# Gate projections between the convolution's projections, scan steps spread over both, and the second gate's tile in one place of the weight ring

## What is computed

```python
h = rms_norm(x, norm_mix)
p = h @ w_in       # columns: conv x | conv B | conv C | ssm u | gate_a | gate_b
gates = sigmoid(gl + gate_bias)
ya = (bg * (causal_conv3(cg * xc) + conv_b)) @ w_conv_out
s_t = a_bar * s_(t-1) + b_bar * u_t          # complex, 32 groups x 64 states
y = gelu(Re(C s_t) + d * u_t)
yb = (y @ w_glu_a) * sigmoid(y @ w_glu_b)
x = x + (gates[0] * ya + gates[1] * yb) @ w_o
x = x + hier_moe(rms_norm(x, norm_ffn))
out = rms_norm(x, norm_final)
```

## Time and profile before

| | before |
|---|---|
| median of 3 runs | 775.52 us |
| lowest, highest | 775.19, 777.94 us |
| span of the profiled execution | 773.0 us |
| TensorE (PE) busy | 625.0 us, 81% |
| VectorE (DVE) busy | 206.9 us, 27% |
| GpSimd (POOL) busy | 92.5 us, 12% |
| ScalarE (ACT) busy | 79.9 us, 10% |
| moved | 242.26 MB, mean 313 GB/s |

### The profile page before, as it was taken

How to read it: one execution, slowest core, us unless ns; L and a number is a source line. 1 busy time by engine, 2 the same in 40 slices (tenths; PEclk the granted TensorE clock), 3 DMA queues, 4 the chain that set the end, 5 groups by cost and what they waited for, 6 DMA issues and landing times.

```text
span 773.0 us, 8709 instructions
## 1 busy us (share of the span) xinstructions
PE 625.0 (81%) x3637; PEld 369.0 (48%) x3637; DVE 206.9 (27%) x415; ACT 79.9 (10%) x150; POOL 92.5 (12%) x92
## 2 busy tenths in 40 slices
PE   7996999599999998989875885794695596597483
PEld 6885778487887664544430341251151152043041
DVE  3969999755301116001010010010000000000002
ACT  3100010013211004100020000020000011000001
POOL 5094636211000001100000000000000000000000
PEclk9998999799999999999998897898898799898887
DMA  8984530822296236899999999999999999999991
GB/s 245 382 278 167 208 120 0 326 109 109 89 410 235 109 135 238 341 409 408 408 410 410 410 409 409 410 410 410 409 409 410 410 409 409 410 410 410 409 380 56
DMA packets 76423, 242.26 MB, mean 313 GB/s; under 512 B 9618, under 2 KB 9710, under 8 KB 76398
## 3 DMA queue, kind: packets, MB, share of 16 engines
q1 hardware_dynamic: 75534, 238.77, 79.3%
q10 hardware_dynamic: 864, 3.15, 1.2%
HBM read 240.86 MB, written 1.05 MB: 313 GB/s over the span
## 4 chain that ended last, share of the span: by engine, by line
PE 41%; DMA 37%; DVE 12%; issue 3%; SPq 3%; POOL 2%; ACT 1%; POOLq 0%; DVEq 0%
PE bank L1077 16%; DMA ring<-in_w_up 15%; DMA ring<-in_w_gate 15%; PE bank L1310 7%; PE bank L1331 4%; PE bank L1189 3%; DMA ring<-in_w_down 3%; DMA rot_region<-in_w_down 3%; SPq L422 3%; PE bank L1055 3%; PE bank L1343 1%; DVE x_region L865 1%; PE bank L1283 1%; DVE x_region L862 1%; DVE conv_region L843 1%
## 5 line engine op out<-in xcount | busy, mean ns | idle before, releaser
L1310 PE MATMUL bank<-ring,z_region 128*32 128x512 f32 x832 | 124.7, 738 | 88.1 <-DMA ring<-in_w_up 54.7
L1077 PE MATMUL bank<-x_region,ring 128*128 128x256 f32 x688 | 154.1, 384 | 0.2 <-DMA ring<-in_w_in 0.2
L1077 PEld LDWEIGHTS bank<-x_region,ring 128*128 128x128 f32 x688 | 130.6, 192 | 22.8 <-issue 4.4
L1310 PEld LDWEIGHTS bank<-ring,z_region 128*32 128x32 f32 x832 | 26.6, 126 | 180.0 <-DMA ring<-in_w_up 73.3
L1055 PEld LDWEIGHTS bank<-ident 128*128 128x128 f32 x496 | 60.3, 199 | 29.9 <-issue 25.5
L1055 PE MATMUL bank<-ident 128*128 128x128 f32 x496 | 65.6, 289 | 4.3 <-POOL ident L465 4.3
L1011 DVE TENSOR_TENSOR z_region<-z_region,bank 128x512 f32<-128x512 f32 x8 | 8.2, 1027 | 220.6 <-ACT z_region L672 220.6
L537 POOL TENSOR_TENSOR stat<-stat,halfneg 128x1 f32<-128x1 f32 x2 | 1.1, 560 | 456.4 <-DVE stat L717 456.4
L1331 PE MATMUL bank<-ring,m_region 128*32 128x512 f32 x320 | 49.0, 741 | 6.1 <-ACT m_region L674 5.5
L1015 DVE COPY m_region<-bank 128x512 f32<-128x512 f32 x8 | 5.5, 691 | 137.4 <-PE bank L1331 137.4
L1077 PE MATMUL bank<-z_region,ring 128*128 128x256 f32 x128 | 31.3, 403 | 8.2 <-DVE z_region L845 8.2
(11 more groups left out here) (231 smaller groups left out, 517.9 us busy)
## 6 DMA issues: line engine op xcount, KB each, us to landing
ring<-in_w_up SPq DMA_DIRECT2D x28, 2048.0 KB, 23.6
ring<-in_w_gate SPq DMA_DIRECT2D x24, 2048.0 KB, 23.5
ring<-in_w_down SPq DMA_DIRECT2D x20, 2048.0 KB, 23.6
ring<-in_w_in SPq DMA_DIRECT2D x11, 2048.0 KB, 13.7
x_region<-in_w_down SPq DMA_DIRECT2D x8, 2048.0 KB, 23.7
rot_region<-in_w_gate SPq DMA_DIRECT2D x4, 2048.0 KB, 23.3
s_region<-in_w_up SPq DMA_DIRECT2D x4, 2048.0 KB, 23.5
rot_region<-in_w_down SPq DMA_DIRECT2D x4, 2048.0 KB, 23.5
```

Of the source, the lines that this page charges most:

```text
L1077: ins = MM(dst, w[:, k, n * P:(n + 1) * P], rhs[:, k, :], start=k == 0, stop=k == kn - 1)
L1310: ins = MM(bank[4 + w % 2][q, :], xT[:, k, q], wt[:, e, 512 * kk:512 * kk + 512], start=k == 0, stop=k == KD - 1)
```

## The change

1. The list is now one of named items (`x`, `b`, `c`, `ga`, `gb`, `co`). Gate A of tile n stands between B and C of tile n + 2, and gate B of tile n behind that C (`GATE_LAG = 2`); gates 6 and 7 follow behind tile 7, and the eight output projections (`co`) come last.
2. The 18 steps stand behind items 4 + 9t // 4, that is every 2.25 items, up to item 42 (before: every 2, up to item 38).
3. Gate A's Sigmoid goes straight into `mixed`; VectorE multiplies it with the output projection out of PSUM. ScalarE's copy of the output projection is gone. The gates use the half bank that x has just been copied out of.
4. Gate B's Sigmoid goes to place 7 of the ring (`gate_b`), since `z_sb` is still in use. The mixer's ring has seven places (`MIX_RING`), the units of the columns come as x, B, C, gate A, gate B for tiles 0 to 3 and then 4 to 7, and the expert unit for place 7 waits for `mixed_ready`. The order of the places for expert units is another, with 7 and then the last mixer unit's place at the end of the ring's.

```diff
-    for g in range(N_MAIN):
-        order.append(("main", g))
-        if g >= 4 and g % 2 == 0 and step < ST + S5_LAG:
+    mains = []
+    for j in range(KD):
+        mains += [("x", j), ("b", j)]
+        mains += [("ga", j - GATE_LAG)] if j >= GATE_LAG else []
+        mains += [("c", j)]
+        mains += [("gb", j - GATE_LAG)] if j >= GATE_LAG else []
+    for n in range(KD - GATE_LAG, KD):
+        mains += [("ga", n), ("gb", n)]
+    mains += [("co", n) for n in range(KD)]
...
+        while step < ST + S5_LAG and g == 4 + step * 9 // 4:
             order.append(("s5", step))
...
+        gate_b = ring[:, MIX_RING, 0:KD * T].rearrange("p (k t) -> p k t", k=KD)
...
-        order = [RING, RING + 1] + [(MIX_UNITS + i) % RING for i in range(RING)] + [RING + 2]
+        order = [RING, RING + 1] + [(MIX_UNITS + i) % MIX_RING for i in range(MIX_RING - 1)] + [MIX_RING, (MIX_UNITS - 1) % MIX_RING, RING + 2]
...
-        U_U, U_XBC, U_CO, U_GA, U_GB, U_GLU, U_WO = 0, 1, 7, 9, 11, (13, 15), (14, 16)
+        U_U, U_PARTS, U_CO, U_GLU, U_WO = 0, {"x": 1, "b": 2, "c": 3, "ga": 4, "gb": 5}, 11, (13, 15), (14, 16)
...
+        def gate_bank(what, n):
+
+            if n + GATE_LAG < KD:
+                return 2 * (n % 2)
+            return 0 if what == "ga" else 2
...
-                if u >= RING:
-                    sp.wait_ge(units_used, u - RING + 1)
+                if u >= MIX_RING:
+                    sp.wait_ge(units_used, u - MIX_RING + 1)
...
+                        elif last < 0 and SLOT_OF[v] == MIX_RING:
+                            sp.wait_ge(mixed_ready, KD)
                         elif last < 0 and SLOT_OF[v] < RING:
-
-                            sp.wait_ge(units_used, MIX_UNITS - RING + v - 1)
+                            sp.wait_ge(units_used, last_mix_unit(SLOT_OF[v]) + 1)
...
+                elif what == "ga":
                     act.wait_ge(ga_psum, n + 1)
-                    if n >= 2:
-                        act.wait_ge(ga_used, n - 1)
-                    nc.scalar.activation(gate[:, n % 2, :], bank[n % 4][:, 0:T], ACT.Sigmoid,
+                    nc.scalar.activation(mixed[:, n, :], bank[gate_bank("ga", n)][:, 0:T], ACT.Sigmoid,
                                          bias=cols[:, R_GATEB + n:R_GATEB + n + 1]).then_inc(ga_ready, 1)
...
+                elif what == "co":
+                    dve.wait_ge(ya_psum, n + 1)
                     dve.wait_ge(ga_ready, n + 1)
-                    V.tensor_tensor(mixed[:, n, :], mixed[:, n, :], gate[:, n % 2, :], ALU.mult).then_inc(ga_used, 1)
+                    V.tensor_tensor(mixed[:, n, :], bank[n % 4][:, 0:T], mixed[:, n, :], ALU.mult).then_inc(ya_ready, 1)
...
+                elif what == "ga":
+                    if n + GATE_LAG < KD:
+                        pe.wait_ge(xs_ready, n + GATE_LAG + 1)
...
+                    if n + GATE_LAG < KD:
+                        pe.wait_ge(ga_ready, n + 1)
...
             pe.wait_ge(y_ready, YB)
-            pe.wait_ge(gb_ready, KD)
             for n in range(KD):
+                if n < 2:
+                    pe.wait_ge(ya_ready, 6 + 2 * n)
```

More of the change, by code:

```diff
@@ L29 @@
 RING = 8
+MIX_RING = 7
 MIX_UNITS = 17
@@ L55 @@
 EVEN_BANKS, ODD_BANKS = (0, 1, 4, 5), (2, 3, 6, 7)
[L57 removed]
 N_LOGITS = NEG + NE
 S5_LAG = 2
+GATE_LAG = 2
 def mixer_schedule():
+    mains = []
[7 more added lines that the diff above has]
+    mains += [("co", n) for n in range(KD)]
     order, step = [], 0
[L66 to L68 removed]
+    for g, main in enumerate(mains):
+        order.append(main)
+        while step < ST + S5_LAG and g == 4 + step * 9 // 4:
             order.append(("s5", step))
             step += 1
[L71 to L73 removed]
+    assert step == ST + S5_LAG
     return order
@@ L308, in mix_slot, with last_mix_unit @@
         def mix_slot(u):
-            return ring[:, u % RING, :]
+            return ring[:, u % MIX_RING, :]
         def transfers_to(slot, units):
-            return sum(2 if u in U_GLU else 1 for u in units if u % RING == slot)
+            return sum(2 if u in U_GLU else 1 for u in units if u % MIX_RING == slot)
+        def last_mix_unit(slot):
+            return max(u for u in range(MIX_UNITS) if u % MIX_RING == slot)
         def mix_loaded(eng, u):
-            eng.wait_ge(loaded[u % RING], 16 * transfers_to(u % RING, range(u + 1)))
+            eng.wait_ge(loaded[u % MIX_RING], 16 * transfers_to(u % MIX_RING, range(u + 1)))
         def w8(u):
@@ L1144, in main @@
-                if g in (11, 23):
-                    owed[0] += 3
-                if g >= 24 and g % 4 == 3:
+                    if n % 4 == 3:
+                        owed[0] += 1
+                    return
+                unit = U_PARTS[what] + 5 * (n // 4)
+                s = 2 * (n % 2)
+                if what == "x":
+                    if n == 0:
+                        pe.wait_ge(cols_ready, 3)
+                    if n >= 2:
+                        pe.wait_ge(z_ready, n - 1)
+                    if n >= 2 + GATE_LAG:
+                        pe.wait_ge(gb_ready, n - 1 - GATE_LAG)
+                    dst, done = bank[s][:, 0:T], xbc_psum
+                elif what == "b":
+                    dst, done = bank[s + 1][:, 0:T], xbc_psum
+                elif what == "c":
+                    dst, done = bank[s + 1][:, T:2 * T], xbc_psum
+                elif what == "ga":
+                    if n + GATE_LAG < KD:
+                        pe.wait_ge(xs_ready, n + GATE_LAG + 1)
+                    else:
+                        pe.wait_ge(gb_ready, KD - GATE_LAG - 1)
+                        pe.wait_ge(ga_ready, n)
+                    dst, done = bank[gate_bank(what, n)][:, 0:T], ga_psum
+                else:
+                    if n + GATE_LAG < KD:
+                        pe.wait_ge(ga_ready, n + 1)
+                    else:
+                        pe.wait_ge(gb_ready, n)
+                    dst, done = bank[gate_bank(what, n)][:, 0:T], gb_psum
@@ L1147, in main @@
+                if (what, n) == ("x", 1):
+                    pe.wait_ge(u_ready, YB)
+                mix_loaded(pe, unit)
+                project(dst, w8(unit), n % 4, hT, done)
+                if n % 4 == 3:
                     owed[0] += 1
```

88 lines of the change are left out of this document (27 added, 61 removed).

## The result

| | before | changed |
|---|---|---|
| median | 775.66 us (4 runs) | 758.46 us (4 runs) |
| lowest, highest | 775.19, 777.94 us | 756.54, 758.73 us |
| span of the profiled execution | 773.0 us | 754.8 us |
| TensorE (PE) busy | 625.0 us, 81% | 615.8 us, 82% |
| ScalarE (ACT) busy | 79.9 us, 10% | 80.9 us, 11% |

The ratio is 0.977, with a 95% interval from 0.975 to 0.979: 17.2 us faster. The forecast was 763.4, with a range down to 761.2, so the kernel is 2.7 us faster than the range allowed. The direction and the mechanism are as forecast; one term of the sum is not, and a second piece, the larger, was not in the sum at all.

What follows compares the result with a forecast made beforehand. TensorE's arrival at the experts, which releases the full-rate expert-unit stream, was taken as the bound. 13.76 - 1.3 - 0.3 = 12.1 us off the 773.0 span gives 760.9, plus 2.5 to the median: 763.4 us, range 761.2 to 768.5.

Steps and rivals of the forecast that it cites:

- What bounds the kernel: Gap-free expert-unit stream from the issue at 315.07, which waits for TensorE; moving TensorE's arrival moves the end by as much.
- What is not changed: Same arithmetic, and the 6.58 us wait before 68.92 for step 1 stays, with the slow clock behind it.
- What goes, 13.76: TensorE waits removed from the mixer, counted from 68.92: 8.20 + 3.36 + 1.59 + 0.61 = 13.76 us.
- the four: Wait before 145.88 (8.20), slow clock after it (3.36), wait before 105.53 (1.59), wait for the last gate's Sigmoid (0.61).
- The cover of the 8.20: Work between C 7 and output projection 0, 19.6 us, hiding the last convolution; cover put at over 10 us.
- What comes, 1.3 + 0.3: New TensorE wait for gate A's Sigmoid before gate B 2, taken as 1.3 us, plus 0.3 for seams.
- The walk to gate B 2: Gate B 2 due at 116.6, gate A's Sigmoid done at 117.7: wait about 1.1 us, between 0 and 3.4.
- The 0.3 for seams: Allowance in the mixer of 0.3 us for seams that a walk does not see.
- no new waits, below 761.7: Rival: no new waits at all and small ones elsewhere gone, 13.8 us or more off; chance 0.05.
- The dearer table switches: Part of the rival that Gelus hold the mixer's gates longer: 767 us, limit 768.4; chance 0.14.
- Late expert units: Rival: early expert units, one fewer in the ring, come late; up to 10.3 us more, 773.7; chance 0.05.
- waits that come back through ScalarE: Rival: VectorE, slowed under GpSimd's rotations, delays Gelus that hold the gates; 785.9 us, slower than before; chance 0.03.

Runs made afterwards that it cites:

- the two-later experiment: Changed kernel with scan steps from step 2 on one or two items later, so two projections stand where TensorE waited 7.1 us: 747.72 us, ratio 0.964.
- The experiment with the gates behind: Changed kernel without interleaving: x, B, C of all eight tiles, then all 16 gate projections, then the output projections: 760.48 us, ratio 0.981.
- The runs with the code shifted: Do-nothing TensorE instructions added: before with 4, 16, 2 more 772.12, 772.61, 772.68 us; changed with 16 more 756.95, with two fewer in all 760.72.

## Why the prediction was right and wrong, step by step

**What bounds the kernel: right.** The stream of expert units is full from the first release on, and the release moved with TensorE's arrival: 14.85 us at the GLU, 14.90 at the release, 14.49 at the last landing.

**What is not changed: right.** The gap at 68 stayed (7.14), with products of 2.08 and a slow pair behind it. That the sum may leave it out was right for a comparison; as the two-later experiment shows, it was the largest thing left in the mixer, and its row had stood there from the start.

**What goes, 13.76: right.** From the products at 68 to the GLU the changed kernel takes 13.95 us less (13.9 over all profiles, the slow pair left out). Each of the four is absent in the timeline of after. The cover of the 8.20 had been put at over 10 us. VectorE ended the last convolution tile at 177.6 and output projection 0 began at 194.63: 17 us. The experiment with the gates behind shows that this step is most of the gain.

**What comes, 1.3 + 0.3: the first step that failed.** Measured are 0 and 0. The place was right. In VectorE's timeline step 4 and the convolution behind it:

```profile
91.43 0.69 DVE L864 TENSOR_TENSOR x_region<-bank,rot_region 128x512 f32<-128x512 f32 x1 [7.53 <-PE bank L1177]
...
92.75 0.92 DVE L868 TENSOR_TENSOR x_region<-x_region 128x256 f32<-128x256 f32 x1
93.60 2.15 DVE L869 TENSOR_TENSOR x_region<-x_region 128x256 f32<-128x256 f32 x1
...
95.78 2.73 DVE L871 TENSOR_TENSOR_SCAN x_region<-s5c,x_region 128x256 f32<-128x256 f32 x1
...
100.45 0.42 DVE L847 TENSOR_TENSOR conv_region<-bank,conv_region 128x256 f32<-128x256 f32 x1
```

beside GpSimd's last three rotations of the third group:

```profile
91.46 1.93 POOL L514 TENSOR_TENSOR rot_region<-s_region 128x1024 f32<-128x1024 f32 x1
93.35 2.11 POOL L515 TENSOR_TENSOR x_region<-s_region 128x1024 f32<-128x1024 f32 x1
95.53 2.42 POOL L516 TENSOR_TENSOR rot_region<-rot_region,x_region 128x1024 f32<-128x1024 f32 x1
```

and ScalarE's, up to the Sigmoid of gate A 2:

```profile
113.34 0.42 ACT L629 ACTIVATE y_region<-y_region 128x256 f32<-128x256 f32 x1 [8.60 <-DVE y_region L888]
113.78 1.28 ACT L614 ACT_TABLE_LOAD   x1
115.07 0.47 ACT L614 ACTIVATE m_region<-bank,cols 128x256 f32<-128x256 f32 x1
```

The chain is the one that was walked: y on VectorE, Gelu, table load, Sigmoid, gate B 2, with the durations of the walk. The Sigmoid ends at 115.54 and gate B 2 starts at 115.60, with nothing idle ahead of it. The walk to gate B 2 was mis-sized in one term: step 4 took 9.02 us (91.43 to 100.45), where I had taken 10.46 from before. The rows show the slowed instructions, 2.15 us for one that takes 0.42 in step 5, 2.73 for a scan of 0.69, and they stop with GpSimd's rotations, at 97.95; VectorE began the step later in them (23.4 us behind the products at 68, before 21.9) and so met fewer. The text had named just this as the lower bound, "0, if the rotations cost step 4 less", and then took a value near the walk. The cover is 0.06 us. That is luck as much as design: the same kind of wait is 1.15 us with the gates behind. The 0.3 for seams had no row and should not have been there; in all mixer timelines of after nothing of that kind shows.

**The last gap: the second step, and the larger.** The sum moves the end with the last landing and takes what follows as fixed ("behind it stand only the last pack's matmuls, the final norm and the store"). It stands in no row of mine, although the chain of before ends with it:

```profile
759.52 5.21 issue
```

An "issue" of 5.21 us in which an engine waits for nothing visible, directly on the path to the end, is a term with two sides. It should have stood in the sum at 0, with a lower bound for the range; the profile of before alone gives none but the whole 5.21. This term alone puts the time outside the range: with no new waits the sum is 13.76, which ends inside it, at 761.7; with the 3.7 that the two profiles show it is 17.5, and the median is 17.2 lower. The runs with the code shifted put the term at 2.2 to 3.2. That the change shortened this gap is luck: two instructions that it adds for another reason happen to shift the code. The step from span to time, 2.5 us in the sum, came out at 3.7 (758.46 and 754.8), since a fast execution was profiled; so the span is 6.1 us below its forecast of 760.9 and the time 4.9 below 763.4.

**Rivals.** The case "no new waits, below 761.7" had 0.05 and is the one that came; by itself it gives 775.5 - 13.8 = 761.7, and the rest to 758.5 is the last gap. The dearer table switches did not show. A load takes 1.28 us in every row, and six fewer of them made no difference that can be told. The Trainium skill, "ScalarE: Activation LUTs", section "Table sets: the hidden batching unit", prices a switch at about 2.7 us, by which the prediction had estimated a time 2.3 us above its forecast; this trace does not agree, for the Gelu ends at 113.76, the load runs from 113.78 to 115.06, and the Sigmoid begins at 115.07. Late expert units and waits that come back through ScalarE did not occur in this kernel; release and landing moved together.

## What to carry to other kernels

Put work that needs nothing of the slow producer between the producer's last part and its consumer, not behind the consumer: the order of the two blocks was worth some 12 us, fine interleaving 1 to 2. Then look at each wait that is left and ask whether the waiting instruction can stand later with something to do ahead of it; moving it by two projections was worth another 10.8 us, with what the slow clock behind it took. And before a few us are put down to an edit, compare the part of the trace that the edit doesn't touch, up to the very last instruction, and run a control that only shifts the code.

## What the runs showed of the hardware that I had not expected

- **TensorE's gap behind the experts' loop has two lengths,** 1.5 to 2.1 and 4.4 to 5.2 us, and two instructions more or fewer far ahead of it decide which. That two instructions which do nothing make a kernel 3.2 us faster is measured (ratio 0.994 to 0.997); why is not.
- **Recovery from an idle stretch differs from one execution to the next.** Behind the gap of 6.1 to 7.3 us at 68, the same pair of projections took 8.47 to 9.92 us in twelve profiles, and 7.17 at full clock. In the router the same stretch took 76.7 or 78.0 to 78.5 us, with the granted clock at 1.00 or 0.91 where the two were compared. Without the gap at 68 the runs' spread fell from 4.0 (eight runs) to 0.57 us (four).
- **VectorE's slowing under GpSimd depends on which of its instructions fall into it.** In step 4 one between two SBUF tiles went from 0.42 to 2.15 us and a scan from 0.69 to 2.73, while one that reads PSUM (L864) took its usual 0.69. Each slowed one ends just behind an instruction of GpSimd: 0.28 us behind 93.39, 0.29 behind 95.46, 0.56 behind 97.95, a little less than each takes alone (0.43, 0.42 and 0.69). That it waits for GpSimd's instruction to end is read from these times and no more. A stretch of VectorE work beside GpSimd therefore has no fixed price; it must be walked instruction by instruction with the start that it will have.
